# The first layer's merge: products straight out of PSUM on the vector engine, with the modulation sums dealt between them

## The reference, cut to what matters

```
def merge(p, ya, yb, yc):
    return (sigmoid(p[13]) * ya + sigmoid(p[14]) * yb + sigmoid(p[15]) * yc) @ w_out

ya = u_conv @ w_conv_out      # (tokens, 512) @ (512, 1024)
yb = (o_gla * silu(g)) @ w_gla_out
yc = (o_att * silu(g)) @ w_attn_out
xs = xs + gate_x * merge(px, ya_x, yb_x, yc_x)
cs = cs + gate_c * merge(pc, ya_c, yb_c, yc_c)
```

```
shift, scale, gate = split(silu(c) @ w_mod[l] + b_mod[l], 3)      # (1024) @ (1024, 3072)
```

## Time and profile before

| | us |
|---|---|
| median of 3 runs | 3383.92 |
| lowest and highest | 3381.69, 3394.71 |
| the profiled execution | 3379.07 |
| its span | 3377.3 |
| mean granted TensorE clock | 0.974 |

### The profile page before, as it was taken

How to read it: one execution, slowest core, us unless ns; L and a number is a source line. 1 busy time by engine, 2 the same in 40 slices (tenths; PEclk the granted TensorE clock), 3 DMA queues, 4 the chain that set the end, 5 groups by cost and what they waited for, 6 DMA issues and landing times.

```text
span 3377.3 us, 40269 instructions
## 1 busy us (share of the span) xinstructions
PE 3191.2 (94%) x15099; PEld 2291.8 (68%) x15099; DVE 1307.8 (39%) x2442; ACT 834.7 (25%) x1479; POOL 1599.3 (47%) x1507
## 2 busy tenths in 40 slices
PE   7999987999999999998989999999999999999988
PEld 4666655656666555465778768888984588889944
DVE  3021325545554412315666543444332334443321
ACT  4123235421111022325411112232110122321110
POOL 1788996000000059961354247775640287765600
PEclk9999989999999999999999999999999999999999
DMA  7111100024444121110234322222221222222211
GB/s 227 40 38 32 38 26 14 14 66 134 125 129 133 40 63 38 44 38 1 72 119 144 96 75 75 63 75 63 76 75 50 64 75 63 76 63 75 74 48 41
DMA packets 259332, 236.59 MB, mean 70 GB/s; under 512 B 20887, under 2 KB 257347, under 8 KB 259141
## 3 DMA queue, kind: packets, MB, share of 16 engines
q1 hardware_dynamic: 259140, 234.02, 22.8%
HBM read 231.91 MB, written 2.10 MB: 69 GB/s over the span
## 4 chain that ended last, share of the span: by engine, by line
PE 83%; DVE 9%; POOL 3%; ACT 3%; issue 2%; DMA 0%; DVEq 0%; ACTq 0%; SPq 0%; POOLq 0%
PE ps L466 29%; PE ps L1140 22%; PE ps L496 10%; PE ps L982 4%; DVE arena L1753 3%; PE ps L1184 2%; ACT arena L1277 2%; PE ps L745 2%; PE ps L1228 1%; PE ps L482 1%; DVE small L1962 1%; DVE bQz L1757 1%; PE ps L1086 1%; POOL arena L2364 1%; PE ps L1220 1%
## 5 line engine op out<-in xcount | busy, mean ns | idle before, releaser
L2364 POOL TENSOR_TENSOR arena<-arena,posi 128x512 f32<-128x512 f32 (+1 forms) x360 | 409.4, 1137 | 30.0
L466 PE MATMUL ps<-hT,wring 128*128 128x512 f32 (+1 forms) x1184 | 411.8, 508 | 1.2 <-ACT arena L1277 1.2
L496 PE MATMUL ps<-hT,wring 128*128 128x512 f32 (+1 forms) x1024 | 373.2, 519 | 1.2 <-ACT arena L1277 1.2
L466 PE MATMUL ps<-arena,wring 128*128 128x512 f32 (+1 forms) x992 | 367.9, 531 | 0.0
L466 PEld LDWEIGHTS ps<-hT,wring 128*128 128x128 f32 x1184 | 230.1, 196 | 169.7 <-issue 153.9
L1277 ACT ACTIVATE arena<-ps 128x256 f32<-128x256 f32 (+4 forms) x403 | 176.4, 438 | 656.2 <-PE ps L466 234.2
L2446 POOL TENSOR_TENSOR arena<-wring 128x512 f32<-128x512 f32 x72 | 92.7, 1288 | 475.5 <-PE ps L1140 292.7
L466 PEld LDWEIGHTS ps<-arena,wring 128*128 128x128 f32 x992 | 187.6, 190 | 175.2 <-issue 168.4
L496 PEld LDWEIGHTS ps<-hT,wring 128*128 128x128 f32 x1024 | 192.5, 192 | 152.3 <-issue 143.5
L1277 ACT ACT_TABLE_LOAD x152 | 195.0, 1283 | 371.8 <-DVE small L2250 85.8
L2363 POOL TENSOR_SCALAR posi<-arena,cols 128x512 f32<-128x512 f32 (+1 forms) x360 | 246.2, 684 | 35.4
(11 more groups left out here) (256 smaller groups left out, 4909.8 us busy)
## 6 DMA issues: line engine op xcount, KB each, us to landing
wring<-in_w_in SPq DMA_DIRECT2D x126, 1024.0 KB, 5.3
wring<-in_w_mod SPq DMA_DIRECT2D x24, 1024.0 KB, 8.3
wring<-in_w_out SPq DMA_DIRECT2D x24, 1024.0 KB, 5.7
wring<-in_w_ada SPq DMA_DIRECT2D x21, 1024.0 KB, 5.2
wring<-in_w_conv_out SPq DMA_DIRECT2D x7, 512.0 KB, 6.1
wring<-in_w_gla_out SPq DMA_DIRECT2D x7, 512.0 KB, 6.2
wring<-in_w_attn_out SPq DMA_DIRECT2D x7, 512.0 KB, 5.5
arena<-in_w_ada SPq DMA_DIRECT2D x3, 1024.0 KB, 5.1
```

The source lines that it names most:

```text
L466: last = eng.matmul(o_(out), a, b_, start=(i == 0), stop=(i == len(parts) - 1))
L496: mm = eng.matmul(bank[b][:, 0:n], w[:, k, j * P:(j + 1) * P], hT[:, k, t0:t0 + n], start=(k == 0), stop=(k == KD - 1))
L2364: pool.link(eng.tensor_tensor(dst, dst, scratch, ALU.add))
```

## The change

ACT copies no output tile any more; it keeps the gates and the evacuation of modulation columns. DVE now walks through the six steps of a round. In steps 3 to 5 it multiplies, tile by tile as TensorE finishes them, the output tile in PSUM with its gate in `mg`, into `mg` in place, and by that frees the bank; behind branch 1 it adds the first two branches. Behind each step it computes the modulation groups that `MOD_LOADS` names for it. The last sum of the round goes from `mg` into `mT` as before. TensorE's and SP's programs are the same.

```diff
@@ ACT, the merge of layer 0
                     for b_ in range(3):
-                        for j in range(2):
-                            for sg in segs(l):
-                                t0, n = SEG[sg]
-                                evac(("mout", l, a, b_, j, sg), my[:, 2 * b_ + j, t0:t0 + n], 0, n)
                         for i in MOD_ENDS[0][3 + b_]:
                             modulate(mods[i][0], [mods[i][1]])
                         act.stage("merge")
@@ DVE, the merge of layer 0
                     for a in range(4):
-                        dve.stage("modulation")
-                        for L, g in mod_groups(l, a):
-                            modulate(L, g)
+                        mods = mod_groups(l, a)
+                        for step in range(6):
+                            dve.stage("merge")
+                            b_ = step - 3
+                            for j in range(2) if b_ >= 0 else ():
+                                eng.wait_ge(*at(("free", ("mgate", l, a, b_, j, last))))
+                                for sg in segs(l):
+                                    s0, n = SEG[sg]
+                                    k = ("mout", l, a, b_, j, sg)
+                                    gate = mg[:, 2 * b_ + j, s0:s0 + n]
+                                    eng.wait_ge(*at(("full", k)))
+                                    tt(gate, bank_of[k][:, 0:n], gate, M_, ("free", k))
+                            if b_ == 1:
+                                tt(mg[:, 0:2, t0:T], mg[:, 0:2, t0:T], mg[:, 2:4, t0:T], A_)
+                            dve.stage("modulation")
+                            for i in MOD_LOADS[0][step]:
+                                modulate(*mods[i])
                         dve.stage("merge")
-                        eng.wait_ge(*at(("free", ("mgate", l, a, 2, 1, last))))
-                        for b_ in range(3):
-                            eng.wait_ge(*at(("free", ("mout", l, a, b_, 1, last))))
-                            tt(my[:, 2 * b_:2 * b_ + 2, t0:T], my[:, 2 * b_:2 * b_ + 2, t0:T], mg[:, 2 * b_:2 * b_ + 2, t0:T], M_)
-                        tt(my[:, 0:2, t0:T], my[:, 0:2, t0:T], my[:, 2:4, t0:T], A_)
-                        tt(mT[:, 2 * a:2 * a + 2, t0:T], my[:, 0:2, t0:T], my[:, 4:6, t0:T], A_, ("merged", l, 2 * a))
+                        tt(mT[:, 2 * a:2 * a + 2, t0:T], mg[:, 0:2, t0:T], mg[:, 4:6, t0:T], A_, ("merged", l, 2 * a))
                         m.mark(("merged", l, 2 * a + 1), *m.at[("merged", l, 2 * a)])
```

## The result

The changed kernel took 3394.13 us (median of 20 runs) against 3389.22 us of the kernel before (20 runs): ratio 1.0019, 95% interval 1.0011 to 1.0027, that is 6.4 us slower (3.7 to 9.2). Forecast were 5.7 us. One of the changed kernel's 20 runs took 6130.11 us at a granted clock of 0.812 and is left out of the ratio. The forecast of 3389.6 us lies 4.5 us under the measured time, because it was counted from the first three runs of the kernel before, whose median was 3383.92; counted from 3389.22, the same 5.7 us give 3394.9.

What follows compares the result with a forecast made beforehand. PE (TensorE), busy for 94% of the span, was taken as the bound; ACT's saving counted 0 and late DVE products 4 x 1.42 = 5.7 us, on the 3383.92 us median: 3389.6 us, range 3381 to 3400.

Steps and rivals of the forecast that it cites:

- the range: Whole kernel's time: 3381 to 3400 us, from 3384 less 3 for scatter to 3396 plus 4.
- the clock rival: Clock falls at each turn of a round, 1.6 us each, 6.4 in all: 3396.0 us; chance 0.12.
- The bound: Four rounds of the stage: PE busy throughout, so DVE and ACT changes matter only where PE waits.
- ACT's 23.5 us: 24 copies of 512 columns and 24 of 256 leave ACT; worth at most 0.2 us, taken as 0.
- the ceiling of 0.2 us: Most the stage could gain: PE's only wait row there, 0.2 us in total, once.
- The walk: DVE's new order per round: late branch 2 products delay PE's four column jobs, about 1.4 us a round.
- The term: PE's delay at each round's end, 1.42 us in each of four rounds, 5.7 us in all.
- The edits costed at nothing: Later weight loads in time, earlier last sum still hidden, PSUM products priced like SBUF ones at 692 ns.
- the earlier merged mark: Round's last sum ends at 892.15 instead of 894.26; the 2 us were hidden before and stay so.
- That DVE slows down beside a busy GpSimd: Rival: modulation x 1.37 slower, 4.6 us more a round, 18.4 in all: 3408.0 us; chance 0.05.
- The signs: Profile after: about sixteen PE waits for DVE, 5 to 6 us; rounds 99.5 us; no DMA wait; clock 1.00.

Runs made afterwards that it cites:

- e1: Changed kernel with modulation group 5 computed on DVE right behind group 4, ahead of branch 1's products; ratio 1.0010 to the kernel before, +3.4 us.
- e5: The changed kernel itself, unaltered, run again beside other runs of the kernel before; ratio 1.0038, +12.8 us.
- e7: Changed kernel with branch 2's first two products between modulation groups 5 and 6 on DVE instead of behind both; ratio 1.0033 to the kernel before, +11.2 us.
- e6: The kernel of e1 (group 5 ahead of branch 1's products) run again; ratio 1.0005 to the kernel before, +1.7 us.
- e3: Changed kernel with modulation group 6 behind branch 2's products instead of ahead of them; ratio 1.0084 to the kernel before, +28.4 us.
- e4: Changed kernel with one more DVE product of 1536 elements a round, result unused, behind the first sum; ratio 1.0069 to the kernel before, +23.3 us.
- e2: Changed kernel's DVE order, but ACT again copies output tiles out of PSUM and products read the copies; ratio 0.9999 to the kernel before, -0.3 us.

## Why the prediction was right

The mechanism held in its parts: where PE waits, for what, and how long. The agreement of the numbers is in part luck. The difference, 6.4 us against 5.7, agrees, but the same kernel gave 12.8 us beside other runs. The time itself, 3394.13 us, lies above the 3386 to 3393 in which I had put the forecast's chance of 0.70; it is inside the range only because this was drawn for the clock rival as well, and it is that high because the three runs that I had counted from were 5.3 us faster than the wider set.

**The bound.** PE alone bounds the stage, and ACT's 23.5 us were worth nothing: e1, with no copies, has a stage 0.40 us shorter than before. That is a little more than the ceiling of 0.2 us that I had read from the waits: the first three rounds themselves became 0.07 to 0.09 us shorter. In the kernel before, the next round's first gate tile takes the bank of the first of the four column jobs; ACT emptied that bank only behind its last copy, from 888.85 to 889.11, and the tile began at 889.25, not ahead of the last job's end as in e1. No wait row names this.

**The walk.** Taken against the changed kernel's own times (PE is 0.22 us ahead of its old times there): group 6 was forecast to end at 887.96 and ended at 887.75 + 0.22; the last product at 890.35, and it was 890.11 + 0.22; a round was to take 99.47 us and took 99.44. The term was 1.42 us a round; the first and second round grew by 1.37 and 1.39 us, the last by 1.31, since most of its old wait of 0.2 us ahead of the output product is gone. On average 1.36, in four rounds 5.45 us against 5.7.

**The edits costed at nothing** held: no wait of PE for a weight load, although group 4's slot was given back later (the issue for branch 2's tiles went from 867.27 to 869.84, 2.8 us later when PE's shift is taken out); the earlier merged mark bought nothing; the products from PSUM cost what SBUF ones cost, 691 ns against the 692 of the earlier trace rows, so the extra overhead on PSUM that the Trainium skill (Perfetto Trace Analysis, "Optimizing Scalar/DVE Operations") gives does not show in the profiled durations here. That DVE slows down beside a busy GpSimd had no occasion: GpSimd stood idle in the four rounds, so that rival was not tried.

**The signs.** The rounds, the end of group 6 and the missing wait for a DMA came out as forecast. The waits did not: I had named four a round and 5 to 6 us in all, and the trace has two a round and 3.7 us, since the other two hide inside pairs of jobs. Nor was the granted clock 1.00 throughout. One reading of mine was off, with nothing hanging on it: at 888.00 three of branch 2's tiles had been full for 1.4 to 6.6 us, not for 0.3 to 7.

**What was mis-sized.** The clock. I had given it as a rival with 1.6 us at each of the four turns, or nothing. It was in between: one turn in four in the first profile, one in four in e5, the last of four in e7, 1.7 us each time. Since it hits some turns only, the expected cost is nearer to 5.4 + 1.7 than to 5.7; the first comparison, 6.4 us (3.7 to 9.2), lies between and cannot tell them apart. And it hits elsewhere by the run: the profiled executions of e1 and e6, one and the same kernel, differ by 4.8 us with a stage of 392.01 us in both, and of the profile's 12.9 us the 5.7 outside the stage were mostly that. The range held, since it reached to the clock rival's 3396.0 plus scatter.

What stays open: whether moving a program by a few us changes how many falls its later stages have on average. The ratios of e5 and e7, whose intervals begin at 7.8 and 7.1 us, would allow some us of that; e6's interval ends at 0.14%. These runs do not settle it.

## What to carry to other kernels

Whoever reads a result out of PSUM also gives the bank back. Moving that duty from an idle engine (ACT waited for PE in 311.8 of the stage's 392 us) to one that works through long groups in order makes every group in its queue a possible wait of TensorE, even if the reading itself is as cheap and the engine is half idle: lay the new order out in time against the bank's next user, not against busy shares. Here moving one group of 4 us ahead of the products that it had blocked was enough to lose nothing.

Where TensorE has no idle time, removing work from the other engines has no price to fetch; and a new wait costs more than its own length where it makes a stretch that brings the clock down, as in e3 and e4.

## What the runs showed of the hardware that I had not expected

In the profiled executions a turn of column jobs and waits of 2.3 us was followed by a fall of the granted clock in three of twelve cases (the changed kernel twice, and e7), with PE at full work before and after; one of 4.1 to 4.3 us (e4) or 5.3 to 5.5 us (e3) in all four of each. The sixteen turns of 0.8 to 1.2 us in the kernel before, e1, e2 and e6 had none. The cost behind one turn was 1.4 to 2.9 us, read from the first 128 matmuls of the round: 41.39 us at full clock, 43.09 in the changed kernel's third round, up to 44.31 in e3. In a turn of 2.3 us PE was idle for only 0.96 us; the rest was column jobs, busy in the rows, which in these three cases did not keep the clock up. The Trainium skill (TensorE: Matmul & The Clock Gate, Part 1) describes the drop after idleness; these turns hold column jobs beside the idle time.

Two executions of one kernel can differ by 10 us and more without any difference in the work: the six runs of e5 span 19 us, while its profiled stage repeated that of the first profile, 399.55 us, to 0.01 us.
